# The even output projection in halves of tokens, and the odd projection's first two units in two passes

## The reference, cut to what matters

```python
# end of the even layer (x: 1024 tokens, xc: 256 context tokens)
x  = x  + gt   * (mix_x @ e_w_out)
xc = xc + gt_c * (mix_c @ e_w_out)
# start of the odd layer; rms(v) = v * rsqrt(mean(v*v) + 1e-6)
hc = rms(xc) * o_norm * (1 + sc_c) + sh_c
h  = rms(x)  * o_norm * (1 + sc)   + sh
k_c, v_c = (hc @ o_w_in)[key and value columns]     # the context needs these 256 columns only
everything = h @ o_w_in                             # 26 units of 128 columns
```

## Time and profile before

| | us |
|---|---|
| median of 3 executions | 2773.04 (2771.98 to 2773.44) |
| the profiled execution, its own time | 2763.63 |
| the profiled execution, its span from first to last instruction | 2761.8 |
| TensorE busy in it | 2509.3 |
| mean granted TensorE clock, share of full speed | 0.954 |

### The profile page before, as it was taken

One profiled execution on the slowest core, in us unless ns is written; L12 is line 12 of the kernel. 1 busy time (PEld: TensorE's weight loads), 2 busy tenths in 40 slices (PEclk: granted clock), 3 DMA queues, 4 the chain that ended last, 5 costly groups with the idle time before them and its releaser, 6 DMA issues.

```text
span 2761.8 us, 28940 instructions
## 1 busy us (share of the span) xinstructions
PE 2509.3 (91%) x11542; PEld 1951.4 (71%) x11542; DVE 1387.0 (50%) x1559; ACT 610.9 (22%) x868; POOL 693.5 (25%) x478
## 2 busy tenths in 40 slices
PE   5998789989899999999996699999996999959998
PEld 3776566667678888888873588874774888738876
DVE  7556644336624344344436699976234022066633
ACT  3012234422411100110124411123104000123310
POOL 1331320035553233233352211100221333210011
PEclk9999879999999999999998899999997999969999
DMA  6651000122232233223221211113310111140001
GB/s 219 200 167 45 21 16 8 46 77 84 62 114 84 76 100 92 81 85 101 81 84 55 84 33 44 38 56 112 103 36 25 46 46 46 38 113 1 1 23 69
DMA packets 220702, 194.31 MB, mean 70 GB/s; under 512 B 15152, under 2 KB 194864, under 8 KB 220336
## 3 DMA queue, kind: packets, MB, share of 16 engines
q1 hardware_dynamic: 214656, 172.25, 20.7%
q0 software_dynamic: 2960, 11.26, 1.1%
q10 hardware_dynamic: 2976, 9.31, 0.9%
HBM read 171.96 MB, written 13.63 MB: 67 GB/s over the span
## 4 chain that ended last, share of the span: by engine, by line
PE 79%; DVE 11%; ACT 3%; issue 3%; PEld 1%; DMA 1%; POOL 1%; PEldq 1%; SPq 1%; DVEq 0%; ACTq 0%; POOLq 0%
PE G L304 29%; PE G L1690 27%; PE M L2697 3%; PE M L307 3%; PE G L1116 2%; DVE WPT L2733 2%; PE M L2682 1%; PE M L1705 1%; PE M L400 1%; PE G L2266 1%; PE M L2266 1%; PE M L1027 1%; PEld G L304 1%; PE G L2293 1%; PE M L1067 1%
## 5 line engine op out<-in xcount | busy, mean ns | idle before, releaser
L304 PE MATMUL G<-HH,WH 128*128 128x512 f32 x1264 | 405.4, 401 | 51.4 <-DVE HL L434 44.1
L304 PE MATMUL G<-HH,WL 128*128 128x512 f32 x1264 | 399.2, 396 | 0.0
L304 PE MATMUL G<-HL,WH 128*128 128x512 f32 x1264 | 399.0, 396 | 0.0
L278 POOL TENSOR_SCALAR WH<-RAW 128x1024 fp32r<-128x1024 f32 (+1 forms) x154 | 134.1, 870 | 874.6 <-PE G L1690 500.7
L281 POOL TENSOR_TENSOR WL<-RAW,WH 128x1024 fp32r<-128x1024 f32 (+1 forms) x154 | 301.6, 1958 | 12.8
L304 PEld LDWEIGHTS G<-HH,WH 128*128 128x128 f32 x1264 | 223.4, 190 | 106.9 <-issue 48.0
L304 PEld LDWEIGHTS G<-HL,WH 128*128 128x128 f32 x1264 | 224.8, 190 | 47.7
L304 PEld LDWEIGHTS G<-HH,WL 128*128 128x128 f32 x1264 | 224.4, 190 | 46.5
L1690 PE MATMUL G<-HH,WH 128*128 128x512 f32 x640 | 227.6, 404 | 13.7 <-POOL WL L281 8.9
L1690 PE MATMUL G<-HH,WL 128*128 128x512 f32 x640 | 224.4, 399 | 0.0
L1690 PE MATMUL G<-HL,WH 128*128 128x512 f32 x640 | 224.2, 399 | 0.0
(11 more groups left out here) (494 smaller groups left out, 4025.4 us busy)
## 6 DMA issues: line engine op xcount, KB each, us to landing
RAW<-in_w_ff SPq DMA_DIRECT2D x40, 512.0 KB, 3.9
RAW<-in_w_ff SPq DMA_DIRECT2D x80, 256.0 KB, 2.5
WVEC<-in_w_ada SPq DMA_DIRECT2D x24, 512.0 KB, 4.6
FVEC<-in_e_w_mod SPq DMA_DIRECT2D x24, 512.0 KB, 4.1
FVEC<-in_o_w_mod SPq DMA_DIRECT2D x24, 512.0 KB, 3.8
RAW<-in_o_w_in SPq DMA_DIRECT2D x24, 512.0 KB, 3.6
RAW<-in_e_w_in SPq DMA_DIRECT2D x20, 512.0 KB, 3.5
ADA<-in_w_ada SPq DMA_DIRECT2D x4, 2048.0 KB, 19.6
```

Source lines behind the costliest of these rows:

```text
L278: pool.tensor_scalar(hi, raw, 1.0, 0.0, ALU.mult, ALU.add).then_inc(w_high, 1)
L304: m = pe.matmul(G[s][:, n * w:(n + 1) * w], part[s][:, k, :], acts[i][:, k, n * w:(n + 1) * w], start=first, stop=last)
```

## The change

`eout`, `ckn`, `ckv` and `on` become one stage `eo` without gates between them.
- It has 18 units. The first eight (`n == 0`) take tokens 0 to 511 and the context, the next eight (`n == 1`) tokens 512 to 1023; each loads and splits its weights anew, so `e_w_out` is loaded and split twice. The last two are the context's keys and values.
- The norm of token half 0, and the context's norm, are spread over the units of half 1. The sum of the context's squares over feature tiles is one strided `tensor_reduce` on VectorE in place of matmuls with ones; its product with the reciprocal, its high part and its low part are one instruction each.
- The norm of half 1 follows after all evictions.
- The lead of `odd` is no longer one unit but two: `odd_first` runs units 0 and 1 on half 0, then both on half 1. The loop that follows starts with unit 2.

The core of the diff, with indentation cut by eight:

```diff
-out_stage("eout", A["e_w_out"], X, lambda f: MODE[:, 16 + f, 0:1], ("ep_lo", range(4), ("ep_g", 6)),
-          side=(XC, lambda f: MODE[:, 16 + f, 1:2], (HHC, HLC)))
...
+EO = [(f, n) for n in range(2) for f in range(KT)]
+SQH = [Z(f"SQH{s}", [P, 512], F32, 2 * s) for s in range(2)]
+NRH = [Z(f"NRH{s}", [P, 512], F32, 8 + 2 * s) for s in range(2)]
+XNH = [Z(f"XNH{s}", [P, 512], F32, 12 + 2 * s) for s in range(2)]
+T32H = [Z(f"T32H{s}", [P, 512], F32, 72 + 2 * s) for s in range(2)]
+CSQ = Z("CSQ", [P, KT, CTX], F32, 20)
+XNC, T32C = Z("XNC", [P, KT, CTX], F32, 52), Z("T32C", [P, KT, CTX], F32, 60)
...
-rms_h("ckn", XC, CTX, 1, 1, gathered=False, sq=[Z(f"CSQ{s}", [P, CTX], F32, 36 + s) for s in range(2)],
-      r=Z("CNR", [P, CTX], F32, 38))
...
+def eo_unit(pe, i, ready=None):
+    f, n = EO[i]
+    U_, s = eo_U(i), i % 2
+    pe.wait_ge(w_split[s], U_ // 2 + 1)
+    need(pe, unit_freed[s], U_ // 2)
+    order = list(range(KT)) if ready is None else list(range(4, KT)) + list(range(4))
+    for j, k in enumerate(order):
+        if ready and k < 4:
+            pe.wait_ge(S(ready), k + 1)
+        for part, a, b in ((WH, HH, HHC), (WH, HL, HLC), (WL, HH, HHC)):
+            first, last = j == 0 and part is WH and a is HH, j == KT - 1 and part is WL
+            m = pe.matmul(G[s][:, half(n)], part[s][:, k, :], a[:, k, half(n)], start=first, stop=last)
+            if n == 0:
+                m = pe.matmul(M[s][:, 0:CTX], part[s][:, k, :], b[:, k, :], start=first, stop=last)
+    m.then_inc(unit_done[s], 1)
...
+def eo_first(pe):
+    pe.wait_ge(S("ep_g"), 6)
+    eo_unit(pe, 0, "ep_lo")
+def on_sum(pe, n):
+    pe.wait_ge(S("on_acc"), 7 * n + 7)
+    pe.matmul(M[0][:, 512 - 512 * n:1024 - 512 * n], ONES[:], NRH[n][:], start=True, stop=True)\
+      .then_inc(S("on_ms"), 1)
+def eo_pe(pe):
+    for i in range(1, len(EO)):
+        eo_unit(pe, i)
+        if EO[i] == (2, 1):
+            on_sum(pe, 0)
+        if EO[i] == (3, 1):
+            pe.wait_ge(S("ck_acc"), 1)
+            pe.matmul(M[1][:, 512:512 + CTX], ONES[:], CNR[:], start=True, stop=True).then_inc(S("ck_ms"), 1)
+    for j in range(2):
+        i = len(EO) + j
+        U_, s = eo_U(i), i % 2
+        if j == 0:
+            pe.wait_ge(S("ck_lo"), 1)
+        pe.wait_ge(w_split[s], U_ // 2 + 1)
+        pe.wait_ge(unit_freed[s], U_ // 2)
+        for k in range(KT):
+            for part, a in ((WH, HHC), (WH, HLC), (WL, HHC)):
+                m = pe.matmul(G[s][:, 0:CTX], part[s][:, k, :], a[:, k, :], start=(k == 0 and part is WH and a is HHC),
+                              stop=(k == KT - 1 and part is WL))
+        m.then_inc(unit_done[s], 1)
+        if j == 0:
+            on_sum(pe, 1)
+    pe.wait_ge(S("ck_v"), 1)
+    for t in range(2):
+        m = pe.transpose(M[1][:, t * P:(t + 1) * P], CV[:, t * P:(t + 1) * P], IDENT[:])
+    m.then_inc(S("ck_tr"), 1)
...
+def eo_dve(dve):
+    def evict(i):
+        f, n = EO[i]
+        unit_ready(dve, eo_U(i))
+        if n == 0:
+            dve.scalar_tensor_tensor(out=XC[:, f, :], in0=M[i % 2][:, 0:CTX], scalar=MODE[:, 16 + f, 1:2],
+                                     in1=XC[:, f, :], op0=ALU.mult, op1=ALU.add).then_inc(S("ck_x"), 1)
+        if n == 0 and f == 4:
+            dve.wait_ge(x_late, 64)
+        dve.scalar_tensor_tensor(out=X[:, f, half(n)], in0=G[i % 2][:, half(n)], scalar=MODE[:, 16 + f, 0:1],
+                                 in1=X[:, f, half(n)], op0=ALU.mult, op1=ALU.add).then_inc(unit_freed[i % 2], 1)
+    def gather(f, n):
+        dve.wait_ge(S("on_sq"), KT * n + f + 1)
+        if f == 0:
+            return
+        if f > 1:
+            dve.wait_ge(S("on_acc"), 7 * n + f - 1)
+        dve.tensor_tensor(NRH[n][:], SQH[0][:] if f == 1 else NRH[n][:], SQH[f % 2][:], ALU.add)\
+           .then_inc(S("on_acc"), 1)
+    def inverse(n):
+        dve.wait_ge(S("on_sd"), n + 1)
+        dve.reciprocal(NRH[n][:], NRH[n][:]).then_inc(S("on_r"), 1)
+        dve.wait_ge(S("on_r"), n + 1)
+    def scaled(f, n):
+        g = KT * n + f
+        if g >= 2:
+            dve.wait_ge(S("on_t32"), g - 1)
+        dve.tensor_tensor(XNH[f % 2][:], X[:, f, half(n)], NRH[n][:], ALU.mult).then_inc(S("on_xn"), 1)
+    def low(f, n):
+        dve.wait_ge(S("on_hi"), KT * n + f + 1)
+        dve.tensor_tensor(HL[:, f, half(n)], T32H[f % 2][:], HH[:, f, half(n)].bitcast(F32), ALU.subtract)\
+           .then_inc(S("on_lo"), 1)
+    dve.wait_ge(moved, info("ef")["dma_end"])
+    dve.wait_ge(xc_back, 16)
+    for i in range(KT):
+        evict(i)
+        if i:
+            gather(i - 1, 0)
+    gather(KT - 1, 0)
+    evict(KT)
+    dve.wait_ge(S("ck_sq"), 1)
+    dve.tensor_reduce(CNR[:], CSQ[:].rearrange("p f n -> p n f"), AX.X, ALU.add).then_inc(S("ck_acc"), 1)
+    for f in (1, 2):
+        evict(KT + f)
+        gather(f - 1, 1)
+    inverse(0)
+    evict(KT + 3)
+    gather(2, 1)
+    dve.wait_ge(S("ck_sd"), 1)
+    dve.reciprocal(CNR[:], CNR[:]).then_inc(S("ck_r"), 1)
+    dve.wait_ge(S("ck_r"), 1)
+    dve.tensor_tensor(XNC[:], XC[:], CNR[:].unsqueeze(1).broadcast_to([P, KT, CTX]), ALU.mult)\
+       .then_inc(S("ck_xn"), 1)
+    scaled(0, 0)
+    for f in range(1, KT):
+        scaled(f, 0)
+        low(f - 1, 0)
+        if f % 2 == 1:
+            evict(KT + 4 + f // 2)
+            gather(3 + f // 2, 1)
+        if f == 5:
+            dve.wait_ge(S("ck_hi"), 1)
+            dve.tensor_tensor(HLC[:], T32C[:], HHC[:].bitcast(F32), ALU.subtract).then_inc(S("ck_lo"), 1)
+    low(KT - 1, 0)
+    gather(KT - 1, 1)
+    inverse(1)
+    scaled(0, 1)
+    for f in range(1, KT):
+        scaled(f, 1)
+        low(f - 1, 1)
+    low(KT - 1, 1)
...
+def eo_act(act):
+    act.dma_start(XC[:], CSPILL).then_inc(xc_back, 16)
+    for f in range(4, KT):
+        act.dma_start(X[:, f, :], SPILL[:, f, :]).then_inc(x_late, 16)
+    def square(f, n):
+        U_ = eo_U(KT * n + f)
+        act.wait_ge(unit_freed[U_ % 2], U_ // 2 + 1)
+        if f >= 2 or n:
+            act.wait_ge(S("on_acc"), 7 * n + max(f - 2, 1) if f >= 2 else 6 + f)
+        act.activation(SQH[f % 2][:], X[:, f, half(n)], ACT.Square).then_inc(S("on_sq"), 1)
+    def root(n):
+        act.wait_ge(S("on_ms"), n + 1)
+        act.activation(NRH[n][:], M[0][:, 512 - 512 * n:1024 - 512 * n], ACT.Sqrt, bias=vec("eps2"), scale=1.0 / D)\
+           .then_inc(S("on_sd"), 1)
+    def tile(f, n):
+        g = KT * n + f
+        act.wait_ge(S("on_xn"), g + 1)
+        if g >= 2:
+            act.wait_ge(S("on_lo"), g - 1)
+        act.activation(T32H[f % 2][:], XNH[f % 2][:], ACT.Identity, bias=MODO[:, f, 0:1], scale=GS[:, 1, f, 0:1])\
+           .then_inc(S("on_t32"), 1)
+        act.wait_ge(S("on_t32"), g + 1)
+        act.activation(HH[:, f, half(n)], T32H[f % 2][:], ACT.Copy).then_inc(S("on_hi"), 1)
+    for f in range(KT):
+        square(f, 0)
+    act.wait_ge(S("ck_x"), KT)
+    act.activation(CSQ[:], XC[:], ACT.Square).then_inc(S("ck_sq"), 1)
+    for f in range(2):
+        square(f, 1)
+    root(0)
+    square(2, 1)
+    act.wait_ge(S("ck_ms"), 1)
+    act.activation(CNR[:], M[1][:, 512:512 + CTX], ACT.Sqrt, bias=vec("eps2"), scale=1.0 / D).then_inc(S("ck_sd"), 1)
+    act.wait_ge(S("ck_xn"), 1)
+    for f in range(KT):
+        for c in range(2 * f, min(2 * f + 2, KT)):
+            act.activation(T32C[:, c, :], XNC[:, c, :], ACT.Identity, bias=MODO[:, c, 1:2],
+                           scale=GS[:, 1, c, 1:2]).then_inc(S("ck_t32"), 1)
+        tile(f, 0)
+        if f % 2 == 1 and f < 7:
+            square(3 + f // 2, 1)
+        if f == 3:
+            act.wait_ge(S("ck_t32"), KT)
+            act.activation(HHC[:], T32C[:], ACT.Copy).then_inc(S("ck_hi"), 1)
+    for f in (6, 7):
+        square(f, 1)
+    root(1)
...
-rms_h("on", X, SEQ, 1, 0)
+        i = len(EO) + j
+        unit_ready(act, eo_U(i))
+        act.activation(dst[:], G[i % 2][:, 0:CTX], ACT.Copy).then_inc(unit_freed[i % 2], 1)
+    U_ = eo_U(len(EO) + 1)
+    act.wait_ge(unit_freed[U_ % 2], U_ // 2 + 1)
+    act.sem_inc(S("ck_v"), 1)
+    for f in range(KT):
+        tile(f, 1)
+    act.wait_ge(S("ck_tr"), 1)
...
+def eo_sp(sp, r0):
+    for i, (f, n) in enumerate(EO + [(0, 2), (1, 2)]):
+        w, c0 = (A["o_w_in"], O_K + P * f) if n == 2 else (A["e_w_out"], P * f)
+        load_unit(sp, (r0 + i) // 2, i % 2, w[:, c0:c0 + P].rearrange("(k p) n -> p k n", p=P), RAW[i % 2][:])
+stage("eo", dict(lead=eo_first, act=eo_act, pe=eo_pe, dve=eo_dve, sp_free=eo_sp), raw=[(len(EO) // 2 + 1, None)],
+      units=len(EO) + 2)
...
+def odd_first(pe):
+    u0 = info("odd")["u0"]
+    for n in range(2):
+        for s in range(2):
+            if n == 0:
+                pe.wait_ge(w_split[s], u0 // 2 + 1)
+                pe.wait_ge(unit_freed[s], u0 // 2)
+            for k in range(KT):
+                if s == 0 and (n or k == 0):
+                    pe.wait_ge(S("on_lo"), KT + k + 1 if n else KT)
+                for part, a in ((WH, HH), (WH, HL), (WL, HH)):
```

(22 more changed lines are left out.)

29 lines of the change are left out of this document (5 added, 24 removed).

## The result

The changed kernel takes 2738.52 us (2735.98 to 2740.62, 4 runs) where the kernel before took 2773.24 beside it: a ratio of 0.9875, interval 0.9858 to 0.9892. That is 34.7 us less where 27.8 were forecast: inside the range of 16 to 38, and just beyond the likeliest part of it, 22 to 34. The profiled execution took 2738.98 us, its span 2737.2.

The account below looks back on a forecast made before the run. TensorE is busy for 91% of the span, so time is won only where it waits, behind the projection. Unit 2 of `odd` moves from 2141.9 to 2114.1, 27.8 us less: 2773.0 - 27.8 = 2745 us, range 2735 to 2757.

Parts of the forecast that it names:

- The projection, 0 us: Output projection in `eo`: TensorE's work stays 111.6 us, units of 8.35 then 5.60 us, so nothing gained or lost.
- The norm beside half 1: Norm of half 0 during half 1's units: one stretch of VectorE work, 57.4 us, taking turns with GpSimd's splits.
- D: Distance from first matmul of `eo`'s lead to first matmul of unit 2 of `odd`: 189.1 us before, forecast 161.3.
- the walk: Forecast's step-by-step timing of `eo_dve` against the other queues, putting the last sum of half 1 at 2083.8.
- The reduction: VectorE's strided sum of the context's squares: priced at 2.3 us, with about 10 us of slack; anything slower, chance 0.03.
- The lead of two units: Start of `odd`: four passes of 5.60 us, 22.4 in all, covering the norm of half 1 with 3 us to spare.
- From there to unit 2: From last sum of half 1 at 2083.8 to unit 2 of `odd`, forecast at 2114.1, low clock and copy TG included.
- One more split before the last sum: End of VectorE's queue in `eo`: tiles 6 and 7, unit 15's eviction, two sums and another GpSimd split, until 2083.8.
- The work after it pays about 2.0: Work behind the cold first context unit: low clock adds about 2.0 us, moving the end of `odd_first` to 2112.9.
- then 3 us: TensorE's second wait, after 7 us before the first context unit: 3 us, for the last sum of half 1.
- VectorE as the bound of the whole stretch: Rival for the norm stretch: each VectorE step pays for signals and turns, 12 to 20 us less; chance 0.17.
- The rival of lighter queues: Rival for the norm stretch: queues lighter than walked, 36 to 39 us less, 2734 to 2737; chance 0.15.

Follow-up runs that it names:

- short splits: Changed kernel with GpSimd splitting only the first of eight k-tiles of the weights for units 8 to 17: D 152.5 us, ratio 0.989 to the kernel before.
- the second measurement: The changed kernel run again unedited, beside the kernel before: medians 2738.57 against 2765.86 us, ratio 0.9901, D 156.1 us.
- Three kernels: Changed kernel with splits of an eighth (D 152.5 us); context's low part one tile earlier (161.2); last sum first, fourth pass after gate, unit 14 evicted early (156.5).

## Why the prediction was right, and where it was off

**The projection, 0 us: right.** Units 1 to 7 keep TensorE busy for 58.72 of 59.30 us, unit 8 ends 0.7 us later than walked. XC, which I had 5.8 us under way, was there 7.7 us after its load began, at 1977.36, with a margin that I had put at 1.7. It cost 0.21 us before unit 2.

**The norm beside half 1: right in mechanism and in size.** The kernel with that norm put behind half 1 is 18.8 us longer in D, and the one with short splits shows that VectorE and GpSimd take turns, as the walk had it. The waits before units 14 and 15 are 0.26 and 0.90 us (forecast 1.1 and 1.3), before the context 6.52 (7).

**The reduction: price wrong, place right.** 3.90 us instead of 2.3, and 2.28 with a read in a row. The Trainium skill, "SBUF — State Buffer", note on cachelines, says that each access that crosses to a new line pays a penalty; the trace agrees in sign, at 1.7 times the price. The slack behind it took up the 1.6 us, as D with the read in a row shows (156.6 both ways); the walk put that slack at 10 us, and VectorE's next three waits for TensorE are 1.03, 4.92 and 1.51.

**The lead of two units: right.** One unit costs 7.3 us more, and the norm of half 1 had its cover: its last low part is ready at 2108.50, ahead of the third pass's last eighth, which starts at 2109.79. That is 1.3 us of cover where the walk had 3.

**From there to unit 2: this is the step that was mis-sized, by 4.2 of the 4.7 us.** It had two terms too many.
- *One more split before the last sum.* The walk put a split in front of the last sum of half 1, and the stretch that holds it came out at 8.4 us in place of 6.0. In the trace the last sum starts at 2088.21 and the split's first operation at 2088.29. A split ahead of that sum fits a context unit of 2.85 us, which is what the walk gave it; it took 4.87, because it ran at the low clock, and so its split came behind the sum.
- *"The work after it pays about 2.0" for the low clock.* It paid nothing: the four passes take 22.6 us where 22.4 + 2.0 were forecast, and the second context unit's matmuls start 0.12 us apart. The low clock ended inside the first context unit (0.50 up to 2087.2, 0.99 from 2087.4 to 2093.6).

The chain and a window of the changed kernel:

```profile
2083.02 4.87 PEld G L2468 x24
...
2083.00:2087.20 4.20, 4.18 (x19) 4.18 (x20) 3.33 (x6) 3.54 (x6) 0.00 (x0) 0.50 0.09 26
```

The Trainium skill, "TensorE: Matmul & The Clock Gate", warns under "Loop structure matters more than you think" that a long wait between matmuls, there for a DMA, lets the array fall to its half-rate clock. The trace agrees for the first context unit, after a wait of 6.52 us: it took 2.0 us more than at full speed, and not the whole 2.9 of a doubling.

The prediction had seen that this unit runs cold, and its wait of "then 3 us" fits that: 2083.8 less 3 is 5.4 us after the unit's start. What it did not do is carry the cold unit into the split behind it. A slower unit costs nothing itself, since TensorE then waits for the last sum anyway. It holds back the split that would have cost something, and it leaves TensorE a wait of only 0.85 us before the ones-sum, behind which the clock stayed up. Three kernels show the other side. With waits of 2.34, 4.75 and 4.95 us before the ones-sum the clock was low again behind it, and in the two of them with whole splits the last sum takes 2.8 us as well: 4.8 us more in one, 3.3 in the other. That a cold unit was needed in the changed kernel is read from the 0.08 us between the last sum and the split; no kernel ran it at full speed in the same place.

The steps that came out were not luck: up to the context's low part each is within 0.7 us. That the second measurement gave 27.3 us, next to the 27.8 of the forecast, is: the medians' gain moved between 27.3 and 34.7 us by itself.

Of the gain of 32.7 us in D (189.1 less the mean 156.4), 18.8 are the norm beside half 1 and 7.3 the lead of two units, each taken back alone; that the two add is not tested. The remaining 6.6 (gates, the context's norm in single operations) were not tried apart. The medians' gains of 34.7, 27.3 and 32.3 us lie about that number. VectorE as the bound of the whole stretch (12 to 20 us less) is ruled out by the gain and by the waits of 0.26 and 0.90 us. The rival of lighter queues (36 to 39 us less) is not what happened either: the queues were as heavy as walked, and what was lighter lies behind them.
